# Turning the experts' rows back from the router's operand: TensorE and ScalarE in GpSimd's place

## What is computed

```python
x = x + mod_l[2] * m_l
h = rms_norm_2(x, norm_ffn[i]) * (1 + mod_l[4]) + mod_l[3]      # modulate
g_logits, e_logits = h @ wg + bg, h @ we + be                   # router: 4 groups x 4 experts
out = sum over the 2 chosen experts of weight * (silu(h @ w_gate) * (h @ w_up)) @ w_down
```

## Time and profile before

| | us |
|---|---|
| three timed runs | 2022.09, 2024.25, 2025.62 (median 2024.25) |
| profiled execution, whole | 2020.34 |
| its span in the trace | 2018.6 |
| PE busy | 1891.2 (94%) |
| DVE busy | 1187.0 (59%) |
| ACT busy | 642.7 (32%) |
| POOL busy | 262.8 (13%) |

### The profile page before, as it was taken

One profiled execution on the slowest core, in us unless ns is written; L12 is line 12 of the kernel. 1 busy time (PEld: TensorE's weight loads), 2 busy tenths in 40 slices (PEclk: granted clock), 3 DMA queues, 4 the chain that ended last, 5 costly groups with the idle time before them and its releaser, 6 DMA issues.

```text
span 2018.6 us, 28998 instructions
## 1 busy us (share of the span) xinstructions
PE 1891.2 (94%) x10950; PEld 1038.5 (51%) x10950; DVE 1187.0 (59%) x1908; ACT 642.7 (32%) x1274; POOL 262.8 (13%) x319
## 2 busy tenths in 40 slices
PE   7999999999999999999998999899997999989993
PEld 4554875544444444555645764633334678645330
DVE  2001777487787653358845644677757667456774
ACT  2011762200000001242313631256643556323551
POOL 3000110011111000012200012611102000051101
PEclk9999999999999999999999999999998989999997
DMA  8632100677666442311111011689965020148995
GB/s 260 169 84 84 54 12 22 219 253 258 235 236 239 147 174 97 133 42 42 42 42 63 1 36 73 266 335 362 363 239 202 1 84 2 35 157 354 387 416 199
DMA packets 108473, 323.89 MB, mean 160 GB/s; under 512 B 9063, under 2 KB 43015, under 8 KB 89904
## 3 DMA queue, kind: packets, MB, share of 16 engines
q1 hardware_dynamic: 77920, 190.56, 26.3%
q0 software_dynamic: 25024, 112.01, 15.6%
q10 hardware_dynamic: 5392, 19.47, 2.4%
HBM read 291.48 MB, written 35.76 MB: 162 GB/s over the span
## 4 chain that ended last, share of the span: by engine, by line
PE 71%; issue 7%; DMA 7%; DVE 6%; PEld 4%; PEldq 2%; ACT 1%; POOL 1%; POOLq 0%; DVEq 0%; SPq 0%; ACTq 0%
PE ps L3441 15%; PE ps L2060 6%; PE ps L466 6%; PE ps L2872 6%; PE ps L1190 5%; PE ps L1236 4%; PE ps L3242 4%; PE ps L1211 4%; DMA X<-moe_rows,row_token 4%; PE ps L364 3%; PE ps L335 2%; PE ps L2893 2%; PE ps L2036 2%; PEld ps L1783 2%; PE ps L1783 1%
## 5 line engine op out<-in xcount | busy, mean ns | idle before, releaser
L3441 PE MATMUL ps<-wide 128*128 128x512 f32 (+1 forms) x736 | 306.5, 575 | 1.9 <-issue 1.7
L3441 PEld LDWEIGHTS ps<-wide 128*128 128x128 f32 x736 | 138.3, 190 | 166.2 <-issue 164.1
L2872 PE MATMUL ps<-wide,X 128*32 x448 | 197.5, 594 | 2.1 <-DVE X L3043 2.1
L2872 PE MATMUL ps<-Z,X 128*32 128x512 f32 x1344 | 197.9, 594 | 0.0
L2060 PE MATMUL ps<-wide 128*128 128x512 f32 (+1 forms) x384 | 148.3, 543 | 0.5 <-issue 0.5
L1544 DVE SCALAR_TENSOR_TENSOR Z<-Z,wide 128x2048 f32<-128x2048 f32 x56 | 131.6, 2349 | 2.8
L1190 PE MATMUL ps<-T 64*128 64x256 f32 (+1 forms) x888 | 109.8, 377 | 8.7 <-DVE nm L1329 6.8
L1783 PE MATMUL ps<-wide 128*128 128x512 f32 x256 | 112.1, 595 | 2.1 <-issue 1.0
L744 ACT ACTIVATE T<-ps 128x512 f32<-128x512 f32 (+2 forms) x139 | 70.7, 536 | 128.2 <-PE ps L1783 109.8
L1261 ACT ACTIVATE T<-T,nm 128x768 f32<-128x768 f32 (+3 forms) x112 | 86.7, 775 | 77.5 <-DVE nm L1329 77.5
L2872 PEld LDWEIGHTS ps<-wide,X 128*32 128x32 f32 x448 | 47.0, 110 | 124.1 <-issue 124.1
(11 more groups left out here) (421 smaller groups left out, 3366.0 us busy)
## 6 DMA issues: line engine op xcount, KB each, us to landing
wide<-in_experts SPq DMA_DIRECT2D x64, 1024.0 KB, 9.7
Z<-in_mod_w POOLq DMA_DIRECT2D x32, 1024.0 KB, 5.2
T<-in_experts SPq DMA_DIRECT2D x32, 1024.0 KB, 11.8
X<-in_mod_w POOLq DMA_DIRECT2D x16, 1024.0 KB, 5.3
moe_out<-X ACTq DMA_DIRECT2D x28, 512.0 KB, 8.5
wide<-in_w_down SPq DMA_DIRECT2D x12, 1024.0 KB, 6.8
wide<-in_w_gate SPq DMA_DIRECT2D x22, 512.0 KB, 6.0
wide<-in_w_up SPq DMA_DIRECT2D x22, 512.0 KB, 6.9
```

Source lines behind the costliest of these rows:

```text
L2872: last = pe.matmul(ps[rows, t % 2, :], mo.xT[:, c, rows], w_rows, start=(c == 0), stop=(c == DK - 1))
L3441: last = pe.matmul(self.gu.bank(u)[:, columns], w, self.rhs(c)[:, columns], start=(c == 0), stop=(c == DK - 1))
```

## The change

The rows are not computed a second time: PE transposes `HT` back to tokens on partitions, in units of half a tile (four transposes of 128x128 into one PSUM bank, `turn`), and ACT copies each unit into the row's place (`copy`); two banks take turns. POOL keeps the storing of `X` and stores the row tiles from a new place in its list. Units 0 to 3 (tiles 0 and 1) are turned in `first_logits`, where idle matmuls were, and copied before ACT takes the last pair; the others are turned after the logits' transposes, where the second lot of idle matmuls was, and copied around and after ACT's exponentials. The loads of gain, shift and scale rows and DVE's joining of them are gone. The load of the rope table moves from POOL's list to ACT's.

```diff
@@ RowAndTileNorm.scalar @@
             if i == ST - 1:
                 act.dma_start(self.away[:, i, :], k.X[:, i, :]).then_inc(k.last_row_stored.sem, 16)
+                for dst, src in self.late:
+                    act.dma_start(dst, src).then_inc(k.last_row_stored.sem, 16)
@@ RowAndTileNorm.gpsimd @@
-            if i == ST - 1:
-                for dst, src in self.late:
-                    pool.dma_start(dst, src).then_inc(k.small_landed.sem, 16)
@@ TileNorm.scalar @@
+        if self.rows_copies:
+            self.rows_copies(act)
         for p in self.rest:
             self.take(act, "act", p)
@@ RowStores @@
+    def turn(self, pe, a, b):
+        k = self.k
+        for u in range(a, b):
+            t = self.norm.tiles[u // 2]
+            if u >= 2:
+                pe.wait_ge(k.rows_copied.sem, self.copied + u - 1)
+            for j in range(4):
+                last = pe.transpose(self.bank(u)[:, j * P:(j + 1) * P], k.HT[:, 4 * (u % 2) + j, t * P:(t + 1) * P], k.ident[:, :])
+            last.then_inc(k.rows_turned.sem, 1)
+    def copy(self, act, a, b):
+        k = self.k
+        for u in range(a, b):
+            act.wait_ge(k.rows_turned.sem, self.turned + u + 1)
+            act.activation(self.place(u // 2)[:, 512 * (u % 2):512 * (u % 2) + 512], self.bank(u), ACT.Copy).then_inc(k.rows_copied.sem, 1)
     def gpsimd(self, pool, ch):
-        for dst, src in self.loads:
-            pool.dma_start(dst, src).then_inc(k.row_mods_landed.sem, 16)
...
-            for c in range(0, D, 256):
-                ch.step(pool.tensor_tensor(row[:, c:c + 256], self.norm.hn[:, t, c:c + 256], gain[:, c:c + 256], ALU.mult))
-            ch.wait()
-            for c in range(0, D, 256):
-                ch.step(pool.tensor_tensor(row[:, c:c + 256], row[:, c:c + 256], shift[:, c:c + 256], ALU.add))
-            ch.wait()
-            pool.dma_start(self.rows_out[t * P:(t + 1) * P, :], row).then_inc(k.rows_stored.sem, 16)
-    def vector(self, dve, ch):
-        k = self.k
-        dve.wait_ge(k.row_mods_landed.sem, self.landed + 16 * len(self.loads))
-        for gain, _ in self.sets:
-            dve.scalar_tensor_tensor(gain, gain, 1.0, self.gain, ALU.add, ALU.mult).then_inc(k.row_gains_ready.sem, 1)
+    def store(self, pool):
+        k = self.k
+        for i, t in enumerate(self.norm.tiles):
+            pool.wait_ge(k.rows_copied.sem, self.copied + 2 * i + 2)
+            pool.dma_start(self.rows_out[t * P:(t + 1) * P, :], self.place(i)).then_inc(k.rows_stored.sem, 16)
@@ Router.gpsimd @@
         self.stores.await_spilled(pool)
         for dst, src in self.rows_gate:
             pool.dma_start(dst, src).then_inc(k.small_landed.sem, 16)
+        self.stores.store(pool)
         self.stores.await_rows(pool)
@@ Router.first_logits, Router.tensor @@
         self.logits(pe, 0)
-        keep_awake(pe, k=self.k, bank=norm.banks.first + 3, n=9)
+        self.stores.last_banks_read(pe)
+        self.stores.turn(pe, 0, self.stores.FIRST)
...
+        self.stores.turn(pe, self.stores.FIRST, 2 * len(self.tiles))
         pe.drain().then_inc(k.places_free.sem, 1)
-        keep_awake(pe, k, 7, 16)
@@ Router.scalar @@
             act.activation(to[:, 0:n, :], x[:, 0:n, :], ACT.Exp).then_inc(k.step_done.sem, 1)
+            if i == 0:
+                self.stores.copy(act, self.stores.FIRST, self.stores.FIRST + 2)
+        self.stores.copy(act, self.stores.FIRST + 2, 2 * n)
```

More of the change, by code:

```diff
@@ L321, in begin, with last_banks_read @@
                 pe.matmul(self.banks.bank(i)[:, 0:cn], self.lhs(k0 + c, t), w[:, c, :], start=(c == 0), stop=False)
+    def last_banks_read(self, pe):
+        self.banks.taken(pe, len(self.blocks) * len(self.tiles) - 2)
     def tensor(self, pe):
@@ L1024, in rows_stored @@
     def rows_stored(self, eng):
-        eng.wait_ge(self.k.small_landed.sem, self.stored + 16 * (ST + len(self.late)))
-        eng.wait_ge(self.k.last_row_stored.sem, self.stored_last + 16)
+        eng.wait_ge(self.k.small_landed.sem, self.stored + 16 * ST)
+        eng.wait_ge(self.k.last_row_stored.sem, self.stored_last + 16 * (1 + len(self.late)))
 class Transposes(Stage):
@@ L2400, with __init__ @@
 class RowStores(Stage):
-    def __init__(self, k, l, norm, gain, mods, rows_out, away):
+    FIRST = 4
+    def __init__(self, k, l, norm, rows_out, away):
         super().__init__(k)
         n = len(norm.tiles)
[L2408 to L2416, removed]
+        self.l, self.norm, self.rows_out, self.away = l, norm, rows_out, away
         self.consts = k.small_landed.reserve(64)
         self.stored, self.spilled = k.rows_stored.reserve(16 * n), k.spilled.reserve(16 * n)
+        self.turned, self.copied = k.rows_turned.reserve(2 * n), k.rows_copied.reserve(2 * n)
         self.n = n
@@ L2506, in tensor @@
         self.stores.norm.pair_taken(pe, len(self.tiles) // 2 - 1)
+        self.stores.await_copied(pe, self.stores.FIRST)
         self.logits(pe, 1)
@@ L3840, in two_blocks, with row_stores @@
         k.expertgate = k.ring[:, 1:3, 1024:SLOT]
-        def row_stores(l, projection, sets):
-            mods = [[bc(scratch["mods"], D, (l * 2 + r) * 6144 + m * D) for m in (3, 4)] for r in range(sets)]
-            projection.row_stores = RowStores(k, l, projection.norm, bc(A["norm_ffn_2"], D, D * l), mods, scratch["h"][l], away)
-            return projection.row_stores
+        def row_stores(l, projection):
+            stores = RowStores(k, l, projection.norm, scratch["h"][l], away)
+            stores.last_banks_read = projection.last_banks_read
+            projection.norm.rows_copies = lambda act: stores.copy(act, 0, stores.FIRST)
+            projection.row_stores = stores
+            return stores
         def moe(l, tiles, head, combine):
@@ L3890, in two_blocks @@
                            norm=mod_sets(0, 1, True))
-        head = [Loading(k, gate_loads(0, 2, 2)), row_stores(0, even.then, 2), even.then]
+        head = [Loading(k, gate_loads(0, 2, 2)), row_stores(0, even.then), even.then]
         oddgate = k.Z[:, 9920:9920 + D].unsqueeze(1)
@@ L3917, in two_blocks @@
         odd.then = Linear(k, hT, DK, A["od_w_out_2"][0], D, seq, gated_take(oddgate), ["dve"] * 8, norm=mod_sets(1, 1, False))
-        moe(1, seq, [row_stores(1, odd.then, 1), odd.then], lambda y, w: Combine(k, seq, y, out[0], w))
+        moe(1, seq, [row_stores(1, odd.then), odd.then], lambda y, w: Combine(k, seq, y, out[0], w))
         def meet(eng, i):
```

13 lines of the change are left out of this document (8 added, 5 removed).

## The result

The changed kernel took 2031.32 us (median of 19 runs, 2025.37 to 2037.88), the kernel before 2023.97 in the same session (19 runs, 2019.91 to 2030.08). The ratio is 1.0034, interval 1.0022 to 1.0046: slower by about 6.9 us (4.5 to 9.3), where +4.2 was forecast. The profiled execution of the changed kernel took 2030.54 us, with a span of 2028.8.

What follows compares the result with a forecast made beforehand. PE's matmuls bound it up to the first logits, then the token list and gather. Rope load -3.5, layer 0 +4.7 and layer 1 +3.0 gave +4.2 us: 2028.5 us, with an 8 in 10 range of 2018 to 2033.

Steps and rivals of the forecast that it cites:

- The rope load: Barrier ahead of the even mixer: falls 1.9 us earlier, and no half-rate clock behind it saves 1.6; together -3.5 us.
- Rival 3: Even mixer's barrier does not move, or the clock falls anyway, and rows are late: about +7 us, 2031; chance 0.10.
- POOL's and DVE's work is worth nothing: Up to the first logits: work taken from POOL and DVE lies beside gapless PE matmuls, so it gains nothing.
- The router's path: Router: turning and copies offset less DVE contention; token list as before in layer 0, about 1 us earlier in layer 1.
- The row stores: Ahead of the first gathers: last landing 1312.5 in layer 0, 1831.5 in layer 1; gathers +3.6 and +2.9 us later.
- the byte bound: Layer 0's last row store: 12.06 MB from 1281.7 at 427 GB/s, landing no earlier than 1309.9.
- The clock behind the first batches: Half clock after PE's idle time ahead of the first batch: +1.1 us in layer 0, +0.5 in layer 1.
- Rivals 1 and 2: Row stores: first, they land under cover, 2018.8, chance 0.20; second, they end with the byte count, about 2023, chance 0.25.
- rival 1: Both layers: row stores land before the token list, which stays the last wait; -5.5 us, 2018.8; chance 0.20.

Runs made afterwards that it cites:

- e1: The kernel before with only the rope load moved from POOL to ACT: 2021.98 us, ratio 0.9977 to the kernel before.
- e2: The changed kernel with the rope load put back on POOL: 2032.95 us, ratio 1.0040 to the kernel before.
- e12: The kernel before with only the rope load moved to ACT, measured again: 2022.55 us, ratio 0.9979 to the kernel before.
- e8: The changed kernel with expert 3's loads held behind the first two gathers and two down weights, and row stores ahead of POOL's wait for X's stores: 2024.66 us.
- e9: The changed kernel with gate and up loads of experts 2 and 3 held until the first two gathers land: 2030.22 us, ratio 1.0025 to the kernel before.
- e11: The changed kernel with row stores ahead of POOL's wait, expert 3's loads held in layer 0 alone, 23 instead of 17 idle matmuls there: 2022.94 us.
- e3: The changed kernel with POOL's row stores ahead of its wait for X's stores to land: 2030.27 us, ratio 1.0020 to the kernel before.
- e4: The changed kernel with gate and up loads of experts 2 and 3 held until all row stores land: 2032.97 us, ratio 1.0036 to the kernel before.
- e7: The changed kernel with only expert 3's gate and up loads held, behind the first two gathers and two down weights: 2025.67 us, ratio 1.0007.
- e13: The kernel before with the rope load on ACT and 23 instead of 17 idle matmuls ahead of layer 0's first batch: 2017.59 us, ratio 0.9962.
- e5: The changed kernel with 42 instead of 17 (layer 0) and 45 instead of 30 (layer 1) idle matmuls ahead of the first batch: 2027.30 us, ratio 1.0018.
- e10: The changed kernel with row stores ahead of POOL's wait in both layers and expert 3's loads held in layer 0 alone: 2023.10 us, ratio 0.9991.

## Why the prediction was right, and where its sizes were off

- **The rope load.** Predicted -1.9 at the barrier and -1.6 in the clock; -1.92 and -1.46 in the profiles, and the timed runs of e1, e2 and e12 agree with the sum. Rival 3 fell, though the measured 2031.3 is its number: ACT reached the barrier with two transfers of its own on the way (issued at 839.56 and 839.95, 5.9 and 6.5 us to landing, while PE went on at 844.11), and the clock stayed up behind it.
- **POOL's and DVE's work is worth nothing.** Right up to the first logits: the projection takes 76.20 us with POOL's arithmetic and without it.
- **The router's path.** "As before in layer 0": the token list came 27.5 us after the first load instead of 28.25. That is a small gain: eight of the ten executions with the turning back have 27.4 to 27.7 (e8 and e9 28.2 to 28.3), the four with the old router 28.25 to 28.45. It is worth nothing while the rows are later than the list. In layer 1 I gave 1 us earlier; it was 26.0 instead of 27.5, but e12, with the old router, also has 26.06, so a gain is not shown there.
- **The row stores.** The term that decides, and right: the last landing at 1312.7 was given as 1312.5, POOL's wake-up by `X`'s landing, given as 1293.5, came at 1293.6, expert 3's loads, near 1298.3, went out at 1297.5. The 1312.5 owes something to luck, though, since the reason that I gave for the distance from the byte bound was wrong (below). In layer 1 the gather came 3.7 us later than before (counted from the first load), 2.9 was given.
- **The clock behind the first batches is the term that was mis-sized.** In layer 0 I charged half rate for the eight transposes alone, +1.1. The clock stayed at half through most of the first batch's matmuls too: the second batch came 11.52 us after the first instead of 9.15, +2.4. In layer 1 I put +0.5; there it was 11.91 instead of 9.09, +2.8. The 1.3 and 2.3 us that I left out are nearly all of the 3.8 by which the two layers (+6.2 and +5.4) exceed the +4.7 and +3.0 forecast.
- **Rivals 1 and 2.** The stores did not land under cover, and the byte bound of 1309.9 was missed by 2.8 us. I had put that down to bandwidth lost while expert 3's loads wait for the turning to end. For 2.5 us from 1299 on queue 1 did have next to nothing, but POOL's queue then filled the engines alone, and 413 GB/s were moved. Queues from 1299 to 1301.5 (packets, MB, share), the sum from 1281.7 to 1309.9, and two windows as above:

```profile
q0 software_dynamic: 272, 0.99, 97.1%
q1 hardware_dynamic: 16, 0.04, 4.6%
...
DMA packets 2026, 11.52 MB, mean 408 GB/s; under 512 B 222, under 2 KB 222, under 8 KB 1020
...
1307.00:1311.00 4.00, 4.00 (x36) 3.77 (x36) 1.08 (x7) 0.00 (x0) 0.00 (x0) 1.00 0.98 400
1311.00:1315.00 4.00, 0.38 (x4) 0.19 (x2) 0.00 (x0) 0.78 (x1) 1.66 (x2) 0.84 0.12 25
```

  What was missing: the mean was 408 GB/s and not 427, so about 0.55 of the 12.06 MB were left at 1309.9. They were moved by 1311, but for 16 packets (0.05 MB) that trickled out while the engines stood nearly idle, up to the landing at 1312.7. What rival 1 promised, had the rows been in time, was -5.5 us; e11, where they are within 1.4 us of the list in layer 0, has -4.1, no more than the rope load alone (-4.3).

The chance went to the right side (slower by over 0.2%), and 2031.3 is inside the range; 3.8 us, nearly all of them the clock, were missing from the sum, and the profile's remaining stretches gave 1.4 us back (-1.1 and -0.4 in the table); no run shows these two to be more than the spread of executions.

## What to carry to other kernels

When a transfer moves to a later place in its queue, ask what is in the engines at that moment: here the same 512 KB took 3 us or 14. In layer 0 an earlier issue (e3) did not help, and the loads that e4, e7 and e9 held back came back as a later wait. Row stores first in both layers, expert 3's loads held in layer 0 alone and a few more idle matmuls (e11) brought both layers back to about where they were before, and no further. Charge an idle time of TensorE not only with its own length but with half of the work behind it for as long as the clock stays down, and look whether a few idle matmuls remove that. And take a change apart before judging it: its smallest part, one load moved to another queue, held all the gain that these runs show.

## What the runs showed of the hardware that I had not expected

- **Packets, not bytes, are shared.** With both queues full, POOL's and SP's got packets one for one (697 and 694 in 18 us), and with it 2.54 and 5.03 MB. Here stores of 3.6 KB a packet beside loads of 7.2 got a third of the bytes, and in layer 0 an issue about 9 us earlier for two of the six (e3) did not bring the last landing forward, counted from the first load. When queue 1 ran dry, POOL's queue alone moved 0.99 MB in 2.5 us.
- **A short idle time is a toss.** Ahead of layer 0's first batch the clock never fell behind 0.56 and 0.82 us (e13, e11), always behind 6.45 to 6.88 (changed, e2, e3, e4), and in four of eight executions behind 1.22 to 2.09: it fell at 1.22, 1.60, 1.88 and 2.09 (e5, e8, e1, e10) and not at 1.66, 1.71, 1.86 and 1.90 (e9, e7, e12, before). What tells these apart is open. My reading of the earlier trace rows, that 1.90 us leave the clock alone, was one throw.
- **A gather among loads** takes 9.8 us instead of 4.8 (e4), with no packet of its queue from 1305 to 1309 us. The row stores of the changed kernel paused in the same way: issued from 1293.63 on, they moved no packet before 1297, while queue 1 filled the engines (1293.6 to 1297: packets, MB, share). Why a transfer of POOL's queue starts so late beside a full queue 1 is open.

```profile
q1 hardware_dynamic: 194, 1.43, 100.1%
```
